# First block's merge as channel rows: gates and branch projections as sums of block products, 256 columns wide; expert 15's last quarters copied by ScalarE

## The reference, cut to what matters

```python
out_a = fox_attention(...) @ w_fox_up            # 512 x 512 @ 512 x 1024
out_b = nsa_attention(...) @ w_nsa_up            # 512 x 512 @ 512 x 1024
mix = sigmoid(g_a) * out_a + sigmoid(g_b) * out_b    # g_a, g_b: columns of h @ w_in
x = x + mix @ w_out
x = x + hierarchical_moe(rms_norm(x, norm_ffn_g), ...)   # 16 experts, two per token
```

## Time and profile before

| what | value |
|---|---|
| median of 3 runs | 1475.31 us (1474.51 to 1477.69) |
| profiled execution | 1475.47 us, span 1474.2 us |
| PE busy | 1394.8 us, 95% of the span |
| DVE, ACT, POOL busy | 38%, 24%, 18% |
| mean granted TensorE clock | 0.977 |
| merge on PE | from 344.83 to 502.42 us |
| w_out's products on PE | from 502.42 to about 552 us |

### The profile page before, as it was taken

The page is one execution under the profiler, slowest core; times in us unless marked ns, Lnnn a source line. Parts: engine busy times, 40 slices in busy tenths (PEclk is TensorE's granted clock), DMA queues, the critical chain, the costliest instruction groups (busy, mean ns, idle before and its releaser), DMA issues. The chain is left out here.

```text
span 1474.2 us, 23732 instructions
## 1 busy us (share of the span) xinstructions
PE 1394.8 (95%) x10084; PEld 747.5 (51%) x10084; DVE 554.3 (38%) x1340; ACT 351.5 (24%) x833; POOL 270.0 (18%) x303
## 2 busy tenths in 40 slices
PE   7998999899999997999999989989999899999997
PEld 5545545565444445444444434446777445655543
DVE  3124423573212534421211143335369382343403
ACT  2225324543101111111111133344211201322221
POOL 3010302204040721122222122010241002111000
PEclk9999999999999998999999999989999999999999
DMA  6164013400312248999999961010140331300311
GB/s 203 58 235 143 1 59 86 150 26 4 113 59 93 101 176 289 318 377 375 379 381 379 392 231 72 8 57 7 52 171 29 82 120 38 123 3 17 117 55 58
DMA packets 98973, 207.78 MB, mean 141 GB/s; under 512 B 14533, under 2 KB 22544, under 8 KB 98736
## 3 DMA queue, kind: packets, MB, share of 16 engines
q1 hardware_dynamic: 87152, 171.38, 32.3%
q0 software_dynamic: 11712, 34.83, 7.1%
HBM read 185.73 MB, written 19.42 MB: 139 GB/s over the span
## 5 line engine op out<-in xcount | busy, mean ns | idle before, releaser
L466 PE MATMUL pb<-Wt,HT 128*128 128x512 f32 (+1 forms) x384 | 152.7, 556 | 1.0 <-DMA Wt<-in_w_in_dram 1.0
L3617 PE MATMUL pb<-Wt,HT 128*128 128x512 f32 x256 | 119.4, 608 | 2.1 <-DVE AR L3708 2.1
L466 PE MATMUL pb<-Wt,AR 128*128 128x512 f32 x256 | 111.5, 592 | 0.0
L466 PEld LDWEIGHTS pb<-Wt,HT 128*128 128x128 f32 x384 | 70.6, 205 | 70.2 <-issue 70.1
L2054 PE MATMUL pb<-AR 128*64 128x512 f32 x256 | 85.0, 595 | 0.7 <-issue 0.7
L678 PE MATMUL pb<-AR 64*128 64x512 f32 (+7 forms) x256 | 65.3, 500 | 14.1 <-ACT AR L773 4.4
L466 PEld LDWEIGHTS pb<-Wt,AR 128*128 128x128 f32 x256 | 48.1, 190 | 57.9 <-issue 57.9
L3617 PEld LDWEIGHTS pb<-Wt,HT 128*128 128x128 f32 x256 | 47.0, 192 | 53.7 <-issue 48.9
L2054 PE MATMUL pb<-Wt,AR 128*64 128x512 f32 x192 | 70.8, 595 | 0.0
L777 ACT ACTIVATE AR<-AR,SM 128x512 f32<-128x512 f32 (+3 forms) x96 | 53.1, 554 | 51.6 <-DVE SM L729 51.2
L729 DVE CUSTOM_DVE_ANT_0 AR<-pb,AR 128x512 f32<-128x512 f32 (+3 forms) x96 | 43.2, 487 | 57.7 <-PE pb L680 57.4
(11 more groups left out here) (562 smaller groups left out, 2363.6 us busy)
## 6 DMA issues: line engine op xcount, KB each, us to landing
Wt<-in_w_in_dram SPq DMA_DIRECT2D x18, 2048.0 KB, 8.6
AR<-in_w_gate_dram SPq DMA_DIRECT2D x8, 2048.0 KB, 18.3
AR<-in_w_up_dram SPq DMA_DIRECT2D x8, 2048.0 KB, 18.7
AR<-in_w_down_dram SPq DMA_DIRECT2D x8, 2048.0 KB, 18.4
Wt<-in_w_gate_dram SPq DMA_DIRECT2D x6, 2048.0 KB, 17.5
Wt<-in_w_down_dram SPq DMA_DIRECT2D x6, 2048.0 KB, 14.4
Wt<-in_w_up_dram SPq DMA_DIRECT2D x6, 2048.0 KB, 21.3
ys<-AR POOLq DMA_DIRECT2D x1, 6144.0 KB, 21.9
```

The lines of the kernel that those rows point to most:

```text
L466: r = mm(s[:, 0:n], lT[:, k, t * 128:(t + 1) * 128], w[:, k, c0:c0 + n], start=k == 0, stop=k == nk - 1)
L3617: r = mm(s, HT[:, k, t * 128:(t + 1) * 128], W.ap(("gate2", c, br))[:, k, :], start=k == 0, stop=k == 7)
```

## The change

- `Quarters` moves ahead of the merge and is made general: its semaphores, tokens, sums, copies and weights are handed to it, and the block height is half the weight's height (h = 4 for gates, h = 2 for branches). The second block uses it as before with shared semaphores.
- The merge becomes eight units of 512 channels by 512 tokens, with channels on partitions: gate c=0, gate c=1, branch c=0, branch c=1, for each b. The branch projections are seven block products as well.
- The turns and `Seven` for the gates are gone. DVE multiplies, and in b=1 adds four times 128 x 512 into `mixT` (which is `HT`) after each branch unit.
- POOL makes 1024-element weight sums for gate units, 512-element ones for branch units, and left sums of `foT` and `noT`.
- `out7` waits for `s_mix`; the first expert loads wait for all eight adds.
- For expert 15 ACT copies all four quarters and frees the bank; DVE only waits for the bank to be full.

```diff
+        class Quarters:
...
+            def right_po(self):
+                t1, t2, t4 = self.rights
+                b = self.before
+                po.wait_ge(*W.loaded(self.name))
+                if b is not None:
+                    po.wait_ge(*b.part(1))
+                gt.tensor_tensor(t1, self.b12, self.b11, ALU.subtract).then_inc(self.right_sem, 1)
+                if b is not None:
+                    po.wait_ge(*b.part(2))
+                po.wait_ge(*self.right(1))
+                gt.tensor_tensor(t2, self.b22, t1, ALU.subtract).then_inc(self.right_sem, 1)
+                gt.tensor_tensor(self.b12, self.b22, self.b12, ALU.subtract).then_inc(self.right_sem, 1)
...
+                    po.wait_ge(*P.filled(b.key("y")))
+                po.wait_ge(*self.right(2))
+                gt.tensor_tensor(t4, self.b21, t2, ALU.subtract).then_inc(self.right_sem, 1)
...
+            def p5_pe(self):
+                pe.wait_ge(self.left_sem, 1)
+                pe.wait_ge(*self.right(1))
+                self.product(P.take(pe, "S", self.key("z")), self.lefts[0], self.rights[0]).then_inc(self.part_sem, 1)
+            def p2_pe(self):
+                pe.wait_ge(*self.first())
...
+            def p3_pe(self):
+                pe.wait_ge(self.left_sem, 3)
+                pe.wait_ge(*self.read(0))
...
+            def p4_pe(self):
+                pe.wait_ge(*self.right(4))
+                pe.wait_ge(*self.read(2))
...
+            def first_ac(self):
+                if self.before is not None:
+                    ac.wait_ge(*P.drained(self.before.key("y")))
+                ac.wait_ge(*self.part(0))
+                st.copy(self.copies[0], self.view("x")).then_inc(self.first_sem, 1)
...
         def merge_po():
             po.wait_ge(s_loc, 1)
-            for b in range(2):
-                gate7[b].right_po()
+            for n, u in enumerate(merge7):
+                u.right_po()
+                if n == 0:
+                    left_sums_po(foT, 2, up_sums, s_uleft[0])
+                if n == 4:
+                    po.wait_ge(*P.filled(merge7[3].key("y")))
+                    left_sums_po(noT, 2, up_sums, s_uleft[1])
 
         def merge_pe():
-            for _ in gate7[0].steps_pe(HT):
-                pass
-            pe.wait_ge(s_loc, 1)
-            for x in uitems:
-                up_go_pe(0, x)
-            for _ in gate7[1].steps_pe(HT):
-                pass
-            for n, x in enumerate(uitems):
-                up_go_pe(1, x)
-                if n > 0:
-                    mix_turn_pe(uitems[n - 1])
+            for n, u in enumerate(merge7):
+                if n == 2:
+                    pe.wait_ge(s_loc, 1)
+                u.p1_pe()
+                if n:
+                    merge7[n - 1].p4_pe()
+                u.p5_pe()
+                u.p2_pe()
+                u.p6_pe()
+                u.p3_pe()
+                u.p7_pe()
+            u.p4_pe()
 
         def merge_ac():
             ac.wait_ge(s_loc, 1)
...
+            for n, u in enumerate(merge7):
+                u.first_ac()
+                if n % 4 < 2:
+                    u.c11_ac(ACT.Sigmoid)
+                    u.rest_ac(ACT.Sigmoid, s_sg)
 
         def merge_ve():
             for b, to in enumerate((mix, sg1)):
...
+                for c in range(2):
+                    g, u = merge7[4 * b + c], merge7[4 * b + 2 + c]
+                    u.p5_ve()
+                    ve.wait_ge(*P.drained(g.key("x")))
+                    ve.wait_ge(*P.filled(u.key("x")))
+                    vt.tensor_tensor(u.c11, u.view("x"), u.c11, ALU.mult).then_inc(P.free(u.key("x")), 1)
+                    u.p6_ve()
...
+                    vt.tensor_tensor(copies[2], u.view("z"), copies[2], ALU.add).then_inc(P.free(u.key("z")), 1)
+                    ve.wait_ge(*P.drained(u.key("z")))
+                    ve.chain(lambda: vt.tensor_tensor(u.c12, u.c12, copies[2], ALU.mult))
+                    ve.wait_ge(*u.read(0))
+                    ve.wait_ge(*u.part(3))
+                    vt.tensor_tensor(copies[1], u.view("y"), copies[1], ALU.add).then_inc(s_read4, 1)
+                    ve.wait_ge(*u.read(2))
+                    ve.chain(lambda: vt.tensor_tensor(u.c22, u.c22, copies[1], ALU.mult))
+                    ve.wait_ge(*P.filled(u.key("y")))
+                    vt.tensor_tensor(up_last, u.view("y"), copies[0], ALU.add).then_inc(P.free(u.key("y")), 1)
...
+                    ve.chain(lambda: vt.tensor_tensor(u.c21, u.c21, up_last, ALU.mult))
+                    ve.after()
                     if b:
...
+                        for m in range(4 * c, 4 * c + 4):
+                            vt.tensor_tensor(mixT[:, m, :], mix[:, m, :], to[:, m, :], ALU.add).then_inc(s_mix, 1)
@@ ffn_norm_pe, ffn_norm_po @@
             def ready(c, i):
-                pe.wait_ge(*P.drained(("mt", (i, c))))
+                pe.wait_ge(s_mix, 4 * c + 4)
...
             out7.right_po()
-            for x in uitems:
-                po.wait_ge(*P.drained(("mt", x)))
+            po.wait_ge(s_mix, 8)
             out7.left_po(mixT)
@@ experts 14 and 15, VectorE and ScalarE @@
                 ve.wait_ge(*P.filled(("yb", b)))
-                if b >= LATE:
+                if b == 15:
+                    return
+                if b == LATE:
...
                     ac.wait_ge(*P.filled(("yb", b)))
-                    for i in range(2, 4):
+                    for i in range(0 if b == 15 else 2, 4):
                         r = st.copy(*last_quarter(b, i))
-                    r.then_inc(s_ycopy, 1)
+                    r.then_inc(P.free(("yb", b)) if b == 15 else s_ycopy, 1)
```

More of the change, by code:

```diff
@@ L311, in build @@
         s_sum7 = sem("product_sums_ready")
+        s_mleft = sem("merge_token_sums_ready")
+        s_uleft = [sem(f"branch{b}_sums_ready") for b in range(2)]
+        s_right4 = sem("weight_sums_ready")
+        s_part4 = sem("block_sum_products_ready")
+        s_first4 = sem("first_block_products_copied")
+        s_read4 = sem("block_sums_read")
         s_sg = sem("merge_gates_ready")
@@ L1483, in build @@
+        mix = Place(AR, ARN, base1).take(8, 512)
+        sg1 = Place(AR, ARN, 8192).take(8, 512)
         mixT = HT
@@ L1496, in build @@
[L1496 to L1502, removed]
+        copies = [ar.take(2, 256) for _ in range(3)]
+        ar = Place(AR, ARN, 25600)
+        quarter_sems = s_part4, s_first4, s_read4, s_right4
+        rights = [ar.take(4, 256) for _ in range(3)]
+        gate_use = dict(sems=(*quarter_sems, s_mleft), tokens=HT, weights=lambda tag: (tag, W.ap(tag)),
+                        lefts=(left_sums[0], left_sums[1], HT[:, 0:4, 256:512], left_sums[2]),
+                        rights=rights, copies=copies, late=None)
@@ new lines, in build @@
+        up_sums = [Place(AR, ARN, x).take(2, 256) for x in (21504, 18432, 18944)]
+        up_last = Place(AR, ARN, 20992).take(2, 256)
+        up_use = [dict(sems=(*quarter_sems, s_uleft[b]), tokens=x, copies=copies, late=None,
+                       weights=lambda tag: (tag[0:2], W.ap(tag[0:2])[:, :, 512 * tag[2]:512 * tag[2] + 512]),
+                       lefts=(up_sums[0], up_sums[1], x[:, 0:2, 256:512], up_sums[2]),
+                       rights=[r[:, 0:2, :] for r in rights]) for b, x in enumerate((foT, noT))]
@@ new lines, in build @@
+        merge7 = []
+        for b, to in enumerate((mix, sg1)):
+            for kind, use in (("gate", gate_use), ("up", up_use[b])):
+                for c in range(2):
+                    tag = ("gate", c, b) if kind == "gate" else ("up", b, c)
+                    merge7.append(Quarters(tag, len(merge7), use, to[:, 4 * c:4 * c + 4, :], False,
+                                           merge7[-1] if merge7 else None))
+        out7 = Seven("wo", 0, 0, [("w_out", c) for c in range(2)], left_sums + right_sums, firsts, None)
@@ L1504, in merge_left_po @@
         def merge_left_po():
             po.wait_ge(*P.filled("cmp1"))
-            gate7[0].left_po(HT)
+            left_sums_po(HT, 4, left_sums, s_mleft)
         def merge_po():
             po.wait_ge(s_loc, 1)
-            for b in range(2):
-                gate7[b].right_po()
[L1514 to L1518, removed]
@@ L1600, in ready @@
             def ready(c, i):
-                pe.wait_ge(*P.drained(("mt", (i, c))))
+                pe.wait_ge(s_mix, 4 * c + 4)
             w = out7.steps_pe(mixT, ready)
-            next(w)
-            mix_turn_pe(uitems[-1])
-            for _ in range(11):
+            for _ in range(12):
                 next(w)
@@ L2891, in build @@
+        feature_use = dict(sems=(*quarter_sems, s_left2), tokens=HT, lefts=token_sums,
+                           rights=weight_sums, copies=(p1s, p5s2, p6s2), late=(s_ob, 4),
+                           weights=lambda tag: (tag, W.ap(tag)))
         units = []
         for n, (tag, dst) in enumerate((("rk", kaT), ("rr", rT), ("rv", vT), ("z_a", oA))):
```

(2 more changed lines are left out.)

285 lines of the change are left out of this document (110 added, 175 removed).

## The result

The changed kernel takes 1485.38 us, median of seven runs (1481.99 to 1495.27), against 1474.51 for the kernel before (seven runs, 1469.34 to 1477.69). The ratio is 1.0065, 95% interval 1.0042 to 1.0089: on 1474.5 us that is 9.6 us slower, between 6.2 and 13.1. The forecast was 1481.4 us with a range of 1468 to 1487, so the median lies in the range and on the forecast's side of zero. The profiled execution of the changed kernel took 1481.99 us, its span 1480.7; the one before spans 1474.2. The two profiles are therefore 6.5 us apart.

What follows compares the result with a forecast made beforehand. The prediction took the merge and experts to be PE-bound. Collision +8.9, clock +2.4 and last expert -5.2 summed to +6.1 us on a median of 1475.31, giving 1481.4 us, range 1468 to 1487.

Steps and rivals of the forecast that it cites:

- Stalls before the collision: Merge's new units: PE waits for sums, copies and reads, 4.3 us in all with the last unit's.
- Unit 0: First gate unit of the merge: p5 waits for POOL's first weight sum, 1.95 us lost.
- the two steps from gate to branch: Merge, units 2 and 6: p2 waits for ACT's copy behind a sigmoid, 0.5 us each.
- E: Merge: end of p4 in the seventh of eight units, predicted 137.8 us after the merge's start, at 482.6.
- The last p4: End of the merge's last unit: no p1 hides the DVE read before this product, 1.0 us.
- The collision: Merge's last unit: DVE's mult and four mixT adds alternate with POOL's w_out sums; w_out's sum product 8.9 us later.
- the sixteen records: PE's p3 and p7 in the merge's last unit, slowed by lower granted clock after idling: 2.4 us, bounds 0 and 3.0.
- z: Start of w_out's first sum product, forecast at E + 42.9 (525.5) before the clock loss of 2.4 us.
- The last expert: Expert 15: ACT's four copies free the bank sooner, shortening PE's wait; 5.2 us gain, bounds 2.2 and 5.2.
- Rival 1: Merge: DVE keeps its turn for all four adds; -3.2 us, 1472.1 us; chance 0.15.
- Rival 2: Merge: no port collision on the path, matmul count decides; -8.6 - 5.2 = -13.8 us, 1461.5; chance 0.15.
- Rival 3: Merge: path meets POOL in more places, four branch units at 1.65 us; +6.1 + 6.6, 1488.0 us; chance 0.10.

Runs made afterwards that it cites:

- merge_only: Kernel before with the new merge alone, experts 14 and 15 copied as before: 1488.66 us, ratio 1.0064.
- sums_wait4: Changed kernel with POOL's sums of w_out held back until the four mixT adds of c=0 are done: 1480.17 us, ratio 1.0009.
- sums_memset: Changed kernel with POOL's four weight sums of w_out replaced by memsets of the same size: 2055.46 us in one run, only the merge read.
- psum_mid: Changed kernel with the branch units' intermediate values left in PSUM, each quarter's add following its own mult: 1470.53 us, ratio 0.9947.
- before_psum: Kernel before with the second branch's mult written into its PSUM bank and the add to mix reading it there: 1474.91 us, ratio 0.9975.

## Why the prediction was right

**Stalls before the collision.** Unit 0 lost 1.66 us (1.95 predicted), the two steps from gate to branch 0.19 each (0.5), and E came 137.60 us after the start (137.8). The seam is shorter than my path for it, which rested on an estimated overlap of 0.53 us with the sigmoid. The last p4 waited 0.88 us (1.0).

**The collision.** In us from E, predicted and measured: the mult of c21 ends at 1.9 and 2.1, the first sum at 6.4 and 6.4, the fourth sum at 21.5 and 21.1, the adds at 22.1 and 21.7, p3 starts at 22.7 and 22.3. The four adds took 19.58 us because one passes after each sum. Then the sixteen records lost 2.4 us to the clock, as taken from the experts' row. z came at 44.8 where 42.9 + 2.4 = 45.3 was worked out, and the profile of merge_only repeats it: adds 19.59 us, idle time 17.00 us. The merge cost 10.6 us for 11.3 predicted. Place, mechanism and size of this step hold, and four kernels show the cause from different sides: the collision moves with the sums (sums_wait4), it goes when POOL stops reading (sums_memset), and it goes when DVE stops needing two SBUF inputs while POOL's sums stay as they are (psum_mid, and before_psum in the old merge).

**The last expert.** This is the term that was mis-sized: 5.2 us taken, 2.6 and 2.8 in two traces, none that the times can tell. I chose the upper bound because a wait of 1.7 us seemed to end before the clock's fall. In six executions the wait has a floor of 2.2 to 2.7 us that I had not seen in the earlier trace rows, where the later DVE covered it, and the clock fell all the same (window 880:882 of the profile after: 0.50).

The first two token blocks lasted 878.40 to 885.96, 7.56 us, against 8.89 before and 5.94 at full clock: of the 3.0 us lost to the clock, 1.3 came back. With 1.3 of the wait this is the 2.6 us. With that term at its measured size my sum would have been 11.3 - 2.6 = +8.7, nearer the 9.6 of the times. The forecast of +6.1 lay 3.5 us below these, so it was right in sign and place by the collision, and too low by this term. The times say +9.5 for the merge alone and nothing for the copies. I can't divide the profiles' 6.5 us and the times' 9.6 further: single executions of one kernel lie 10 us and more apart.

**Rival 1**, DVE keeping its turn, said 4 us of idle time and z at E + 33.9. The changed kernel shows 17 us and E + 44.8 with four adds queued without a wait between them, so it falls. **Rival 2** falls for the changed kernel, as the load was there and POOL's first sum ran behind t4 of unit 7. But the price that it named, 8.6 us of gain in the merge, is what psum_mid measures when the collision is taken out: 8.5. The count of matmuls was sound; the gain was there and was lost again in one collision. **Rival 3**, more meetings in the other branch units, did not come: of the 137.60 us to E, 134.8 are records and 2.04 the stalls named above, which leaves 0.8 us for every other meeting in seven units.

## What to carry to other kernels

When a change turns scattered small DVE operations into a run of them, look at what POOL does at that moment: each one with two SBUF inputs can cost a whole POOL instruction, and everything queued behind the run pays for it. Before reordering either engine, ask whether one input can stay in PSUM; here this made a change that lost 9.6 us into one that wins 7.8. Read a wait's floor from an execution in which the named releaser was early, before booking the whole wait as gain.

## What the runs showed of the hardware

- Sums of 128x2048 take 4.51 us alone and 4.82 to 4.96 beside adds with two SBUF inputs, so POOL loses under half a microsecond a turn while DVE, at 4.88 to 4.98 us for an add of 0.6, loses over four.
- Behind an idle time of 2.69 us at the last expert the granted clock stood at 0.50 (window 880:882); behind one of 1.39 us in the merge of psum_mid it stayed at 1.00 (window 494:497), and p4's eight records took 1.97 us.
- A DVE operation that reads and writes the same PSUM bank (0.70 us for 128x512) costs what one into SBUF does (0.69 us).
- Executions of one kernel scatter with PE's mean granted clock: over the 35 runs of the kernel before, the times fall by about 13 us for 0.01 of clock, with a correlation of -0.93 (0.984 at 1470.0 us, 0.974 at 1487.3). Over the 22 runs it is 9.5 us and -0.82. Most of the 17 us between the shortest and the longest of the 35 runs go with the clock in this way; which causes the other no run shows. Effects of 3 us stayed open here for that scatter.
